# A hybrid attention layer with the compressed branch's padding to 128 taken out: 15-wide transposes and 15-row products in place of zero-filled 128-wide ones

## The chip, the cores and the metric

One core of one Trainium2 chip. The metric is the device time of one execution in microseconds (us). Of several executions the median counts.

## What is computed

One layer that is half block attention (MoBA, 8 heads) and half NSA attention (8 heads in 2 groups), on 256 tokens of width 2048, all in float32. With 256 tokens there is a single MoBA block, and the four selection blocks of NSA are all taken, so both the selected and the window branch are plain causal attention over 256 keys. The third NSA branch attends to 15 compressed tokens. Cut to what matters here:

```python
h = rmsnorm(x, g_norm)
proj = jnp.einsum('bsd,de->bse', h, w_in)          # 2048 x 7704
# NSA: n_cmp = 15 compressed keys and values per group
k_c = compress_tokens(n_kc..., pe_ck, w_ck1, w_ck2)
v_c = compress_tokens(n_vc..., pe_cv, w_cv1, w_cv2)
s_c = jnp.einsum('bgrqd,bgnd->bgrqn', q_raw, k_c).astype(jnp.float32) * scale
p_c = masked_softmax(s_c, cmp_end[None, :] <= pos[:, None])
o_c = jnp.einsum('bgrqn,bgnd->bgrqd', p_c.astype(v_c.dtype), v_c)
...
return gates[..., 0:1] * o_c + gates[..., 1:2] * o_s + gates[..., 2:3] * o_w
...
y = jnp.concatenate([y_moba, y_nsa], axis=-1)
return x + jnp.einsum('bse,ed->bsd', y, w_out)     # then a last rmsnorm
```

## The kernel before

The kernel is written engine by engine: each of SyncE, GpSimd, TensorE, ScalarE and VectorE has its own list of instructions, in an order written out by hand, and they meet at semaphores.

**The large products.** The input projection has 15 chunks of 512 columns, each cut into 4 units of 4 x 128 contraction rows; the output projection has 4 chunks, 16 units. This makes 76 slots, and `unit(slot)` runs in each. The weights of a unit arrive by a 1 MB DMA in `w_raw`; ScalarE rounds them to `w_hi` (`hi`, line 683) two slots ahead, VectorE takes the rest as `w_lo` (`lo`, line 879), and TensorE runs three products for each pair of operands (`three_products`, lines 420 to 422): 24 matmuls of 512 columns in a slot. In `matmul(out, a, v)` the argument `a` is the stationary side, loaded into the array by a LDWEIGHTS, and `v` streams past it.

**The attention** hangs between these units. There are 24 jobs (`JOBS`): 16 for NSA, two per head (b = 0 the selected branch, b = 1 the window branch), in slots 20 to 35, and 8 for MoBA after that. A job goes through four slots:
- slot s: `scores(j)` on TensorE (lines 573, 574 and, for the compressed keys, 577) into bank `b_s`; `row_max(j)` on VectorE into `prob`.
- slot s+1: `exps(j)` on ScalarE (line 741), `normalise(j)` on VectorE.
- slot s+2: `prob_T(j)` on TensorE transposes the probabilities into bank `b_p`, 128 columns at a time (line 588): four transposes for an NSA job, three for a MoBA job; `prob_out(j)` on ScalarE copies them to `pT` (line 748).
- slot s+3, for the second job of a head: `values(j)` on TensorE multiplies with the values into bank `b_o` (line 616); `o_evac(j)` on VectorE copies the result out.

In `prob[:, j % 2]` columns 0 to 383 hold the two causal pieces and columns 384 to 398 the 15 compressed probabilities of the 128 queries of half b; columns 399 to 511 are zero padding. So the fourth transpose is 128 x 128 with 113 zero rows in its result, and the product with the compressed values (line 614) has a contraction of 128 of which 113 are zero; rows 15 to 127 of `vc` are zero as well. The zeros are written by GpSimd: `vc` and one half of `prob` at the start (lines 346, 347), the other half of `prob` before projection chunk 5 (line 366), since that half first holds the second-layer weights `w2`. The semaphore `pad_ok` says that they are there; TensorE waits for it before the first transpose and ScalarE before it writes `vc`.

TensorE's order in a slot is: the unit, a transpose round of a projection chunk (`round_`, line 406), `values`, `prob_T`, `scores`. [...] Before the attention some small products use a part of the array: `ck_unit` (line 514) and `gates` (line 551) have 32 stationary columns, `ck_layer2` (line 539) has 15, and the first transpose (line 647) has 16 rows.

Of the kernel before, what the change touches and what calls it, by code (L numbers as in the profile page):

```python
# [134 lines left out]
CK2_SLOT = [12, 18]  # L135
GATE_SLOT = 13
TP = 2 * CS
PAD_CHUNK = 5

Y_ROUNDS = {54: [(0, 0, 0)], 55: [(0, 0, 1)], 56: [(0, 1, 0)], 57: [(0, 1, 1)],  # L140
            62: [(1, 0, 0), (1, 0, 1)], 63: [(1, 1, 0), (1, 1, 1)]}
# [10 lines left out]
def build_layer(nc, x, positions, inv_freq, w_in, g_norm, pe_ck, pe_cv, w_ck1, w_ck2, w_cv1, w_cv2,  # L152
# [4 lines left out]
    with ExitStack() as ctx:  # L157
        def sb(name, shape, dt=F32):
            return ctx.enter_context(nc.sbuf_tensor(name, shape, dt))
# [20 lines left out]
        raw_e = sb("raw_e", [P, MT, CW])  # L180
        junk = raw_e[:, :, :].rearrange("p m c -> p (m c)").bitcast(BF16)

        prob = sb("prob", [P, 2, 4 * P])
        w2 = prob[:, 0, :].rearrange("p (v t d) -> p v t d", v=2, t=2)


        pT = sb("pT", [P, 2, 512])
# [13 lines left out]
        sel = sb("sel", [P, 32])  # L201
        gate, gate_j = sb("gate", [P, MT, NGATE]), sb("gate_j", [P, NH, 2, 4])
        hid_e, hidT = sb("hid_e", [P, 2, TP]), sb("hidT", [P, 2, 2, TP])
        kcT, vc = sb("kcT", [P, CS + P]), sb("vc", [P, NG, HD])
        ssy, rstdy = sb("ssy", [P, 2, MT, 2]), sb("rstdy", [P, 2, MT])
        ssf, ssf1, rstdf = sb("ssf", [P, MT, 4]), sb("ssf1", [P, MT]), sb("rstdf", [P, MT])

# [15 lines left out]
        ident_ok, consts_ok, pool_step = sem("ident_ok"), sem("consts_ok"), sem("pool_step")  # L223
        sel_ok, xlo_even, rstd_ok, rope_sum, y_done = sem("sel_ok"), sem("xlo_even"), sem("rstd_ok"), sem("rope_sum"), sem("y_done")
        rstdy_ok, rstdf_ok = sem("rstdy_ok"), sem("rstdf_ok")
        gmul, pad_ok = sem("gmul"), sem("pad_ok")

        crows_T, x_round, unit_used, t_round = sem("crows_T"), sem("x_round"), sem("unit_used"), sem("t_round")
        ck_used, ck_sum, ck2_done = sem("ck_used"), sem("ck_sum"), sem("ck2_done")
# [91 lines left out]
        @block.gpsimd  # L321
        def _(pool):
            steps = [0]

            def link(ins):

                steps[0] += 1
                ins.then_inc(pool_step, 1)
                pool.wait_ge(pool_step, steps[0])


            link(nc.gpsimd.memset(ident[:, :], 0.0))
            nc.gpsimd.affine_select(out=ident[:, :], in_=ident[:, :], compare_op=ALU.not_equal, fill=1.0, base=0,
                                    pattern=[[-1, P]], channel_multiplier=1).then_inc(ident_ok, 1)
            nc.gpsimd.memset(half_c[:, :], -0.5)
            link(nc.gpsimd.memset(mask[:, :], 0.0))
            for c0, n, step, base in ((0, P, -1, 0), (2 * P, P, -1, 0), (3 * P, NCMP, -CS, 1 - CL), (3 * P + 16, NCMP, -CS, P + 1 - CL)):
                nc.gpsimd.affine_select(out=mask[:, c0:c0 + n], in_=mask[:, c0:c0 + n], compare_op=ALU.is_ge, fill=NEG,
                                        base=base, pattern=[[step, n]], channel_multiplier=1).then_inc(consts_ok, 1)
            link(nc.gpsimd.memset(sel[:, :], 0.0))  # L340
            for n in range(4):
                link(nc.gpsimd.affine_select(out=sel[:, :], in_=sel[:, :], compare_op=ALU.not_equal, fill=1.0, base=-32 * n,
                                             pattern=[[-1, 32]], channel_multiplier=1))
            nc.gpsimd.memset(kcT[:, TP:], 0.0).then_inc(sel_ok, 1)
            nc.gpsimd.memset(KV8[:, D:], 0.0).then_inc(sel_ok, 1)
            nc.gpsimd.memset(vc[:, :, :], 0.0).then_inc(pad_ok, 1)
            nc.gpsimd.memset(prob[:, 1, 3 * P + NCMP:], 0.0).then_inc(pad_ok, 1)

            for r in range(0, 8, 2):
                q, m = r // 2, r % 2  # L350
                pool.wait_ge(xhi_done, r + 1)
                nc.gpsimd.tensor_tensor(xT_lo[:, q * UK:(q + 1) * UK, m * P:(m + 1) * P],
                                        x_buf(r),
                                        xT_hi[:, q * UK:(q + 1) * UK, m * P:(m + 1) * P].bitcast(F32),
                                        ALU.subtract).then_inc(xlo_even, 1)

            pool.wait_ge(sq_done, 2)
            link(nc.gpsimd.tensor_scalar(ssx[:, :], ssx[:, :], 1.0 / D, EPS, ALU.mult, ALU.add))
            nc.gpsimd.tensor_tensor(rstd[:, :], ssx[:, :], half_c[:, :], ALU.pow).then_inc(rstd_ok, 1)
            pool.wait_ge(rstd_ok, 1)  # L360
            nc.gpsimd.tensor_scalar(nrstd[:, :], rstd[:, :], -1.0, None, ALU.mult).then_inc(rstd_ok, 1)

            for i, kind in enumerate(KINDS[:NC]):
                if i == PAD_CHUNK:
                    pool.wait_ge(ck2_done, 2)
                    nc.gpsimd.memset(prob[:, 0, 3 * P + NCMP:], 0.0).then_inc(pad_ok, 1)
                if kind in ROPED:
                    w = 2 * HD if kind == "kv" else CW
                    for m in range(MT):
                        pool.wait_ge(dve_read, dve_reads(i - 1) + 2 * (m + 1))  # L370
                        nc.gpsimd.tensor_tensor(rope_a[:, m, 0:w], rope_a[:, m, 0:w], rope_b[:, m, 0:w],  # L371
                                                ALU.add).then_inc(rope_sum, 1)
                elif kind == "z":
                    n = CHUNKS[i][2]
                    z = (rope_a, rope_b)[n % 2]
                    if n == 0:
                        pool.wait_ge(o_out, 2 * NH)
                    for m in range(MT):
                        pool.wait_ge(dve_read, dve_reads(i - 1) + m + 1)
                        nc.gpsimd.tensor_tensor(xo[:, m, n * CW:(n + 1) * CW], xo[:, m, n * CW:(n + 1) * CW],  # L380
                                                z[:, m, :], ALU.mult).then_inc(y_done, 1)
                    if n % 2:
                        h = n // 2
                        pool.wait_ge(y_sq, 4 * (h + 1))
                        link(nc.gpsimd.tensor_tensor(rstdy[:, h, :], ssy[:, h, :, 0], ssy[:, h, :, 1], ALU.add))
                        link(nc.gpsimd.tensor_scalar(rstdy[:, h, :], rstdy[:, h, :], 1.0 / HW, EPS, ALU.mult, ALU.add))
                        nc.gpsimd.tensor_tensor(rstdy[:, h, :], rstdy[:, h, :], half_c[:, :], ALU.pow).then_inc(rstdy_ok, 1)

            pool.wait_ge(gfin_in, 16)
            for c in range(3):  # L390
                for m in range(MT):
                    pool.wait_ge(fin_sq, 2 * c + m + 1)
                    nc.gpsimd.tensor_tensor(acc[:, m, c * CW:(c + 1) * CW], acc[:, m, c * CW:(c + 1) * CW],  # L393
                                            g_fin[:, c * CW:(c + 1) * CW], ALU.mult).then_inc(gmul, 1)
            pool.wait_ge(ssf_ok, 2)
            for m in range(MT):
                pool.wait_ge(fin_sq, 7 + m)
                one = slice(m, m + 1)
                link(nc.gpsimd.tensor_scalar(ssf1[:, one], ssf[:, m, 3:4], 1.0 / D, ssf1[:, one], ALU.mult, ALU.add))
                nc.gpsimd.tensor_tensor(rstdf[:, one], ssf1[:, one], half_c[:, one], ALU.pow).then_inc(rstdf_ok, 1)  # L400

        @block.tensor
        def _(pe):
# [177 lines left out]
            def prob_T(j):  # L581
                pe.wait_ge(prob_ready, j + 1)
                if j:
                    pe.wait_ge(pt_out, j)
                if j == 0:
                    pe.wait_ge(pad_ok, 3)
                for n in range(4 if JOBS[j][1] == "nsa" else 3):
                    last = nc.tensor.transpose(b_p[:, n * P:(n + 1) * P], prob[:, j % 2, n * P:(n + 1) * P], ident[:, :])  # L588
                last.then_inc(pt_done, 1)

            def values(j):
# [10 lines left out]
                for m in range(MT):  # L602
                    prods = []
                    if kind == "moba":
                        for kt in range(m + 1):
                            prods.append((pT[:, j % 2, (m + kt) * P:(m + kt + 1) * P], mv[:, kt, h * HD:(h + 1) * HD]))
                    else:
                        g = h // 4
                        for br in range(2):
                            jb = j - 1 + br  # L610
                            for kt in range(m + 1):
                                prods.append((pT[:, jb % 2, (m + kt) * P:(m + kt + 1) * P], nv[:, br, kt, g * HD:(g + 1) * HD]))
                        jb = j - 1 + m
                        prods.append((pT[:, jb % 2, 3 * P:4 * P], vc[:, g, :]))
                    for n, (a, v) in enumerate(prods):
                        last = nc.tensor.matmul(b_o[:, m * P:(m + 1) * P], a, v, start=n == 0, stop=n == len(prods) - 1)  # L616
                last.then_inc(pv_done, 1)
# [60 lines left out]
        def _(act):  # L678
# [65 lines left out]

            def prob_out(j):
                act.wait_ge(pt_done, j + 1)
                n = (4 if JOBS[j][1] == "nsa" else 3) * P
                nc.scalar.activation(pT[:, j % 2, 0:n], b_p[:, 0:n], ACT.Copy).then_inc(pt_out, 1)  # L748

            def quarters_out(n):  # L750

# [9 lines left out]

            def ck2_evac(kv):
                act.wait_ge(ck2_done, kv + 1)
                if kv:
                    act.wait_ge(pad_ok, 2)
                if kv == 0:
                    nc.scalar.activation(kcT[:, 0:TP], b_o[:, 0:TP], ACT.Copy).then_inc(ck2_out, 1)
                else:
# [392 lines left out]
```

## Time and profile before

| what | value |
|---|---|
| median of 3 executions | 517.62 us (517.52 to 518.07) |
| profiled execution, whole | 517.52 us |
| its span, first to last instruction | 515.7 us |
| TensorE matmul (PE) busy | 504.7 us, 98% |
| VectorE (DVE) busy | 292.7 us, 57% |
| ScalarE (ACT) busy | 238.5 us, 46% |
| GpSimd (POOL) busy | 62.8 us, 12% |
| mean granted TensorE clock | 0.996 of full |

The whole time is 1.8 us more than the span; that difference lies outside the kernel's instructions. PE is the matmul row, PEld the weight loads, which overlap it. Ends of matmuls are modelled, so what is read of PE below is the distance between the starts of neighbouring records, not their durations.

### The profile page before, as it was taken

How to read it: one execution, taken by the hardware profiler on the slowest of the kernel's cores; microseconds unless marked ns; L12 is line 12 of the kernel's file. 1: busy time of each engine (PE TensorE's matmuls, PEld its weight loads, DVE VectorE, ACT ScalarE, POOL GpSimd, SP SyncE). 2: the span in 40 equal slices, each digit the busy share in tenths (PEclk: the TensorE clock that was granted, in tenths of full speed). 3: DMA queues.
4: the chain of work that ended last, by engine and by line, in shares of the span. 5: the costliest groups of instructions: out<-in, count | busy, mean ns of one | idle time of the engine just before them, and what ended most of it. 6: DMA issues, size and time to landing. Idle time of an engine off the chain costs nothing.

```text
span 515.7 us, 6584 instructions
## 1 busy us (share of the span) xinstructions
PE 504.7 (98%) x2616; PEld 419.3 (81%) x2616; DVE 292.7 (57%) x512; ACT 238.5 (46%) x346; POOL 62.8 (12%) x69
## 2 busy tenths in 40 slices
PE   7999999999999999999999999999999999999993
PEld 6878777777888888888888888888888888888882
DVE  3797343445364766665665675555366666645541
ACT  3685343334445454364445444545463552545421
POOL 3210101001020300300012030001131030011020
PEclk9999999999999999999999999999999999999998
DMA  8898579584435244344334334443985457265313
GB/s 287 290 299 313 181 256 343 201 325 164 163 129 198 83 163 165 102 143 160 128 122 163 101 145 164 164 163 125 370 303 170 161 177 241 85 244 205 123 42 122
DMA packets 53903, 96.46 MB, mean 187 GB/s; under 512 B 4240, under 2 KB 13040, under 8 KB 53488
## 3 DMA queue, kind: packets, MB, share of 16 engines
q1 hardware_dynamic: 50688, 95.43, 53.0%
q10 hardware_dynamic: 3184, 0.61, 0.6%
q8 instruction: 21, 0.34, 0.3%
q14 instruction: 10, 0.08, 0.0%
HBM read 93.93 MB, written 2.10 MB: 186 GB/s over the span
## 4 chain that ended last, share of the span: by engine, by line
PE 97%; DMA 1%; DVE 0%; ACT 0%; DVEq 0%; POOLq 0%; issue 0%; SPq 0%; POOL 0%
PE proj L420 27%; PE proj L422 27%; PE proj L421 27%; PE b_o L616 4%; PE b_t L406 2%; PE b_s L574 2%; PE b_p L588 2%; PE b_s L514 2%; PE b_s L573 1%; DMA xo<-in_x_dram 1%; PE b_t L640 1%; PE b_s L577 1%; PE b_o L551 1%; PE b_o L406 0%; PE b_p L406 0%; PE b_o L539 0%
## 5 line engine op out<-in xcount | busy, mean ns | idle before, releaser
L879 DVE TENSOR_TENSOR w_lo<-w_raw,w_hi 128x2048 fp32r<-128x2048 f32 x72 | 167.0, 2322 | 103.6 <-ACT w_hi L683 103.1
L420 PE MATMUL proj<-w_hi,xT_hi 128*128 128x512 f32 x536 | 215.2, 401 | 0.1
L422 PE MATMUL proj<-w_hi,xT_lo 128*128 128x512 f32 x536 | 209.6, 391 | 0.0
L421 PE MATMUL proj<-w_lo,xT_hi 128*128 128x512 f32 x536 | 209.1, 390 | 0.0
L683 ACT ACTIVATE w_hi<-w_raw 128x2048 fp32r<-128x2048 f32 x72 | 137.4, 1910 | 44.4 <-PE proj L422 35.4
L420 PEld LDWEIGHTS proj<-w_hi,xT_hi 128*128 128x128 f32 x536 | 100.8, 188 | 22.8 <-issue 3.4
L422 PEld LDWEIGHTS proj<-w_hi,xT_lo 128*128 128x128 f32 x536 | 100.7, 188 | 21.5
L421 PEld LDWEIGHTS proj<-w_lo,xT_hi 128*128 128x128 f32 x536 | 101.0, 188 | 19.5
L371 POOL TENSOR_TENSOR rope_a<-rope_a,rope_b 128x512 f32<-128x512 f32 (+1 forms) x16 | 26.2, 1661 | 243.0 <-DVE rope_b L949 243.0
L735 ACT ACTIVATE Q<-b_t 128x512 f32<-128x512 f32 x18 | 10.8, 598 | 62.0 <-PE b_t L406 62.0
L748 ACT ACTIVATE pT<-b_p 128x512 f32<-128x512 f32 (+1 forms) x24 | 13.4, 557 | 53.8 <-PE b_p L588 53.8
L741 ACT ACTIVATE prob<-prob,nmx 128x128 f32<-128x128 f32 (+2 forms) x64 | 25.8, 407 | 0.2 <-DVE nmx L995 0.2
L991 DVE CUSTOM_DVE_ANT_0 prob<-b_s,mask 128x128 f32<-128x128 f32 (+2 forms) x64 | 16.7, 307 | 15.5 <-PE b_s L577 10.5
L420 PE MATMUL proj<-w_hi,ymT_hi 128*128 128x512 f32 x64 | 25.0, 391 | 0.0
L422 PE MATMUL proj<-w_hi,ymT_lo 128*128 128x512 f32 x64 | 25.0, 390 | 0.0
L421 PE MATMUL proj<-w_lo,ymT_hi 128*128 128x512 f32 x64 | 24.9, 390 | 0.0
L1004 DVE TENSOR_SCALAR coef<-sums 128x3 f32<-128x3 f32 (+1 forms) x24 | 4.5, 187 | 26.1 <-ACT prob L741 26.1
L1009 DVE TENSOR_SCALAR prob<-prob,coef 128x128 f32<-128x128 f32 (+2 forms) x64 | 15.5, 295 | 0.8
L380 POOL TENSOR_TENSOR xo<-xo,rope_a 128x512 f32<-128x512 f32 x4 | 7.2, 1812 | 70.6 <-DVE xo L1016 54.2
L1016 DVE COPY xo<-b_o 128x256 f32<-128x256 f32 x16 | 6.8, 422 | 15.2 <-PE b_o L616 15.2
L393 POOL TENSOR_TENSOR Q<-Q 128x512 f32<-128x512 f32 x6 | 7.6, 1291 | 62.6 <-ACT raw_e L790 62.6
L790 ACT ACTIVATE raw_e<-Q 128x512 bf16<-128x512 f32 x8 | 5.0, 631 | 21.6 <-DVE Q L1056 21.3
(163 smaller groups left out, 438.9 us busy)
## 6 DMA issues: line engine op xcount, KB each, us to landing
w_raw<-in_w_in_dram SPq DMA_DIRECT2D x57, 1024.0 KB, 4.9
w_raw<-in_w_out_dram SPq DMA_DIRECT2D x16, 1024.0 KB, 5.0
xo<-in_w_ck_dram SPq DMA_DIRECT2D x4, 1024.0 KB, 5.7
xo<-in_w_cv_dram SPq DMA_DIRECT2D x4, 1024.0 KB, 5.5
w_raw<-in_w_in_dram SPq DMA_DIRECT2D x12, 256.0 KB, 6.8
Q<-in_x_dram SPq DMA_DIRECT2D x1, 2048.0 KB, 10.1
out_dram<-Q SPq DMA_DIRECT2D x4, 512.0 KB, 3.2
xo<-in_x_dram SPq DMA_DIRECT2D x3, 512.0 KB, 8.0
```

Source lines behind the costliest of these rows:

```text
L371: nc.gpsimd.tensor_tensor(rope_a[:, m, 0:w], rope_a[:, m, 0:w], rope_b[:, m, 0:w], ALU.add).then_inc(rope_sum, 1)
L420: nc.tensor.matmul(dst, a_hi, b_hi, start=first, stop=False)
L421: nc.tensor.matmul(dst, a_hi, b_lo, start=False, stop=False)
L422: return nc.tensor.matmul(dst, a_lo, b_hi, start=False, stop=last)
L616: last = nc.tensor.matmul(b_o[:, m * P:(m + 1) * P], a, v, start=n == 0, stop=n == len(prods) - 1)
L683: nc.scalar.activation(split_of(u)[0], w_raw[:, u % RAW], ACT.Copy).then_inc(hi_ready, 1)
L735: nc.scalar.activation(dst, src, ACT.Copy).then_inc(t_out, 1)
L741: last = nc.scalar.activation(prob[:, b, c0:c1], prob[:, b, c0:c1], ACT.Exp, bias=nmx[:, b, n:n + 1], scale=SCALE, accum_out=sums[:, b, n: ...
L748: nc.scalar.activation(pT[:, j % 2, 0:n], b_p[:, 0:n], ACT.Copy).then_inc(pt_out, 1)
L879: nc.vector.tensor_tensor(wl, w_raw[:, u % RAW], wh.bitcast(F32), ALU.subtract).then_inc(lo_ready, 1)
L991: nc.vector.tensor_tensor_reduce(out=prob[:, j % 2, c0:c1], in0=b_s[:, c0:c1], in1=mask[:, k0:k0 + c1 - c0], scale=1.0, scalar=NEG, op0=AL ...
L1009: last = nc.vector.tensor_scalar(prob[:, j % 2, c0:c1], prob[:, j % 2, c0:c1], coef[:, j % 2, i:i + 1], None, ALU.mult)
```

## The change

The padding goes. `prob` shrinks from 2 x 512 to 2 x 400 columns (`w2` then lies across both halves, long before the first job), `vc` from 128 to 16 partitions, the three GpSimd fills go with the semaphore `pad_ok` and every wait on it. In an NSA job the fourth transpose takes 15 columns of `prob` and writes 15 partitions of `b_p`. `prob_out` becomes two copies for an NSA job: 128 partitions x 384, and 15 partitions x 128. The product with `vc` gets a contraction of 15 in place of 128. Nothing of the arithmetic result changes: what is left out was multiplied by zero.

```diff
-        prob = sb("prob", [P, 2, 4 * P])
+        prob = sb("prob", [P, 2, 400])
-        w2 = prob[:, 0, :].rearrange("p (v t d) -> p v t d", v=2, t=2)
+        w2 = prob[:, :, :].rearrange("p a b -> p (a b)")[:, 0:4 * HD].rearrange("p (v t d) -> p v t d", v=2, t=2)
...
-        kcT, vc = sb("kcT", [P, CS + P]), sb("vc", [P, NG, HD])
+        kcT, vc = sb("kcT", [P, CS + P]), sb("vc", [16, NG, HD])
...
-            nc.gpsimd.memset(vc[:, :, :], 0.0).then_inc(pad_ok, 1)
-            nc.gpsimd.memset(prob[:, 1, 3 * P + NCMP:], 0.0).then_inc(pad_ok, 1)
...
-                if i == PAD_CHUNK:
-                    pool.wait_ge(ck2_done, 2)
-                    nc.gpsimd.memset(prob[:, 0, 3 * P + NCMP:], 0.0).then_inc(pad_ok, 1)
...
-                if j == 0:
-                    pe.wait_ge(pad_ok, 3)
-                for n in range(4 if JOBS[j][1] == "nsa" else 3):
+                for n in range(3):
                     last = nc.tensor.transpose(b_p[:, n * P:(n + 1) * P], prob[:, j % 2, n * P:(n + 1) * P], ident[:, :])
+                if JOBS[j][1] == "nsa":
+                    last = nc.tensor.transpose(b_p[0:NCMP, 3 * P:4 * P], prob[:, j % 2, 3 * P:3 * P + NCMP], ident[:, :])
...
-                        prods.append((pT[:, jb % 2, 3 * P:4 * P], vc[:, g, :]))
+                        prods.append((pT[0:NCMP, jb % 2, 3 * P:4 * P], vc[0:NCMP, g, :]))
...
-                n = (4 if JOBS[j][1] == "nsa" else 3) * P
-                nc.scalar.activation(pT[:, j % 2, 0:n], b_p[:, 0:n], ACT.Copy).then_inc(pt_out, 1)
+                last = nc.scalar.activation(pT[:, j % 2, 0:3 * P], b_p[:, 0:3 * P], ACT.Copy)
+                if JOBS[j][1] == "nsa":
+                    last = nc.scalar.activation(pT[0:NCMP, j % 2, 3 * P:4 * P], b_p[0:NCMP, 3 * P:4 * P], ACT.Copy)
+                last.then_inc(pt_out, 1)
...
             def ck2_evac(kv):
                 act.wait_ge(ck2_done, kv + 1)
-                if kv:
-                    act.wait_ge(pad_ok, 2)
```

TensorE's list at the first `values`, in slot 24, before (`b_o` is the values' bank, `b_p` that of the transposes, `b_s` that of the scores; a row is output, stationary or streamed inputs, shape of the output):

```order
L616 MATMUL b_o<-nv,pT 128x128 x2
L616 MATMUL b_o<-vc,pT 128x128
L616 MATMUL b_o<-nv,pT 128x128 x4
L616 MATMUL b_o<-vc,pT 128x128
L588 MATMUL b_p<-ident,prob 128x128 x4
L573 MATMUL b_s<-Q 128x128
L574 MATMUL b_s<-Q 128x256
L577 MATMUL b_s<-kcT,Q 128x128
```

The same place with the change:

```order
L610 MATMUL b_o<-nv,pT 128x128 x2
L610 MATMUL b_o<-vc,pT 128x128
L610 MATMUL b_o<-nv,pT 128x128 x4
L610 MATMUL b_o<-vc,pT 128x128
L580 MATMUL b_p<-ident,prob 128x128 x3
L582 MATMUL b_p<-ident,prob 15x128
L567 MATMUL b_s<-Q 128x128
L568 MATMUL b_s<-Q 128x256
L571 MATMUL b_s<-kcT,Q 128x128
```

No instruction of TensorE moves or goes. The two `vc` products keep their output and lose 113 rows of contraction, which the rows don't show, and each stands between products that use the whole array. [...]

ScalarE's list in a slot with an NSA job, before (`w_hi` is the rounding of a unit's weights, for two slots later):

```order
L741 ACTIVATE prob,sums<-prob,nmx 128x128
L741 ACTIVATE prob,sums<-prob,nmx 128x256
L741 ACTIVATE prob,sums<-prob,nmx 128x15
L748 ACTIVATE pT<-b_p 128x512
L683 ACTIVATE w_hi<-w_raw 128x2048
```

And with the change:

```order
L735 ACTIVATE prob,sums<-prob,nmx 128x128
L735 ACTIVATE prob,sums<-prob,nmx 128x256
L735 ACTIVATE prob,sums<-prob,nmx 128x15
L741 ACTIVATE pT<-b_p 128x384
L743 ACTIVATE pT<-b_p 15x128
L677 ACTIVATE w_hi<-w_raw 128x2048
```

One copy has become two, ahead of the next rounding. It is so 16 times. GpSimd's list loses its three fills and is otherwise the same; VectorE's and SyncE's are the same.

## Rows read from the trace of the kernel before

**Rows 1.** The page: busy time, and the chain that ended last.

```profile
PE 504.7 (98%) x2616; PEld 419.3 (81%) x2616; DVE 292.7 (57%) x512; ACT 238.5 (46%) x346; POOL 62.8 (12%) x69
...
PE 97%; DMA 1%; DVE 0%; ACT 0%; DVEq 0%; POOLq 0%; issue 0%; SPq 0%; POOL 0%
```

**Rows 2.** Waits of PE, all of them: total us, times, longest.

```profile
PE b_t L640 <- POOL ident L333: 1.5, 1, 1.5
PE b_s L406 <- DMA xo<-in_x_dram: 0.8, 1, 0.8
PE b_o L406 <- DMA xo<-in_x_dram: 0.6, 1, 0.6
```

**Rows 3.** Busy time by stage: window; PE, PEld, DVE, ACT, POOL; clock, DMA share.

```profile
148.00:297.00 149.00, 149.00 (x819) 128.49 (x818) 94.19 (x276) 73.52 (x158) 14.06 (x8) 1.00 0.40 137
```

**Rows 4.** PE in order of time, ends of slots 22 and 23 (start us, us, what).

```profile
163.06 0.60 PE L406 MATMUL b_t<-ident,raw_e 128*128 128x128 f32 x4
163.50 0.60 PE L588 MATMUL b_p<-ident,prob 128*128 128x128 f32 x4
163.93 0.39 PE L573 MATMUL b_s<-Q 128*128 128x128 f32 x2
164.16 0.60 PE L574 MATMUL b_s<-Q 128*128 128x256 f32 x2
164.59 0.39 PE L577 MATMUL b_s<-kcT,Q 128*128 128x128 f32 x2
164.73 0.48 PE L420 MATMUL proj<-w_hi,xT_hi 128*128 128x512 f32 x1
165.04 0.40 PE L421 MATMUL proj<-w_lo,xT_hi 128*128 128x512 f32 x1
165.28 0.40 PE L422 MATMUL proj<-w_hi,xT_lo 128*128 128x512 f32 x1
...
170.74 0.60 PE L588 MATMUL b_p<-ident,prob 128*128 128x128 f32 x4
```

**Rows 5.** PE in order of time, the first values, slot 24.

```profile
178.16 0.61 PE L616 MATMUL b_o<-nv,pT 128*128 128x128 f32 x4
178.61 0.39 PE L616 MATMUL b_o<-vc,pT 128*128 128x128 f32 x2
178.83 1.06 PE L616 MATMUL b_o<-nv,pT 128*128 128x128 f32 x8
179.72 0.39 PE L616 MATMUL b_o<-vc,pT 128*128 128x128 f32 x2
179.95 0.60 PE L588 MATMUL b_p<-ident,prob 128*128 128x128 f32 x4
```

**Rows 6.** PE in order of time, where line 539's 15-wide products stand.

```profile
136.51 0.60 PE L406 MATMUL b_t<-ident,raw_e 128*128 128x128 f32 x4
137.04 1.04 PE L539 MATMUL b_o<-prob,hidT 128*15 128x128 f32 x8
138.02 0.50 PE L420 MATMUL proj<-w_hi,xT_hi 128*128 128x512 f32 x1
138.35 0.39 PE L421 MATMUL proj<-w_lo,xT_hi 128*128 128x512 f32 x1
```

**Rows 7.** PE in order of time, around line 514's 32-wide products.

```profile
53.78 0.39 PE L422 MATMUL proj<-w_hi,xT_lo 128*128 128x512 f32 x1
54.09 1.10 PE L514 MATMUL b_s<-xo,KV 128*32 128x256 f32 x16
55.13 0.50 PE L420 MATMUL proj<-w_hi,xT_hi 128*128 128x512 f32 x1
55.47 0.39 PE L421 MATMUL proj<-w_lo,xT_hi 128*128 128x512 f32 x1
55.70 0.40 PE L422 MATMUL proj<-w_hi,xT_lo 128*128 128x512 f32 x1
...
124.56 0.50 PE L420 MATMUL proj<-w_hi,xT_hi 128*128 128x512 f32 x1
124.89 0.39 PE L421 MATMUL proj<-w_lo,xT_hi 128*128 128x512 f32 x1
```

**Rows 8.** PE in order of time, the 16-row transpose near the start.

```profile
6.50 0.63 PE L406 MATMUL b_o<-ident,xo 128*128 128x128 f32 x2
...
6.71 0.42 PE L406 MATMUL b_o<-ident,xo 128*128 128x128 f32 x1
7.07 0.28 PE L647 MATMUL b_p<-ident,pT 16*128 16x16 f32 x1
```

**Rows 9.** Loads of line 616: min, median, max ns, first and last start.

```profile
L616 PEld LDWEIGHTS b_o<-vc,pT x32: 191/192/193, 178.5 to 289.1; 128*128 128x128 f32 x32
```

**Rows 10.** PE groups by shape: busy us, mean ns, idle before.

```profile
L616 PE MATMUL b_o<-vc,pT 128*128 128x128 f32 x32 | 6.2, 276 | 0.0
L514 PE MATMUL b_s<-xo,KV 128*32 128x256 f32 x128 | 8.8, 393 | 0.0
L539 PE MATMUL b_o<-prob,hidT 128*15 128x128 f32 x8 | 1.0, 274 | 0.0
```

**Rows 11.** ACT groups by shape: busy us, mean ns, idle before and its releaser.

```profile
L748 ACT ACTIVATE pT<-b_p 128x512 f32<-128x512 f32 x16 | 9.5, 591 | 30.8 <-PE b_p L588 30.8
L748 ACT ACTIVATE pT<-b_p 128x384 f32<-128x384 f32 x8 | 3.9, 489 | 23.1 <-PE b_p L588 23.1
L769 ACT ACTIVATE vc<-b_o 15x256 f32<-15x256 f32 x1 | 0.4, 372 | 0.4 <-PE b_o L539 0.4
```

**Rows 12.** ACT in order of time, slot 23.

```profile
165.36 0.57 ACT L748 ACTIVATE pT<-b_p 128x512 f32<-128x512 f32 x1
165.84 1.91 ACT L683 ACTIVATE w_hi<-w_raw 128x2048 fp32r<-128x2048 f32 x1
```

**Rows 13.** DVE in order of time, slot 23.

```profile
167.77 2.29 DVE L879 TENSOR_TENSOR w_lo<-w_raw,w_hi 128x2048 fp32r<-128x2048 f32 x1
```

**Rows 14.** POOL in order of time, its fills and what follows.

```profile
4.60 0.31 POOL L346 MEMSET vc<- 128x256 f32 x1
4.85 0.19 POOL L347 MEMSET prob<- 128x113 f32 x1
9.03 1.29 POOL L352 TENSOR_TENSOR xT_lo<-rope_a,xT_hi 128x512 fp32r<-128x512 f32 x1 [3.99 <-ACT xT_hi L693]
```

More of the change, by code:

```diff
@@ L137 @@
 TP = 2 * CS
-PAD_CHUNK = 5
 Y_ROUNDS = {54: [(0, 0, 0)], 55: [(0, 0, 1)], 56: [(0, 1, 0)], 57: [(0, 1, 1)],
@@ L225, in build_layer @@
         rstdy_ok, rstdf_ok = sem("rstdy_ok"), sem("rstdf_ok")
-        gmul, pad_ok = sem("gmul"), sem("pad_ok")
+        gmul = sem("gmul")
         crows_T, x_round, unit_used, t_round = sem("crows_T"), sem("x_round"), sem("unit_used"), sem("t_round")
```

## The prediction

> **What bounds the kernel now.** I read the page first. PE is busy in 98% of the span, and the chain that ended last is PE for 97% [rows 1]. That alone doesn't say that PE is at its limit, since a busy PE can be a slow one, so I read its waits next: three, 2.9 us in all, each in the first microseconds [rows 2]. [...] The question is what the new shapes do to the distance between PE's starts.
>
> **The yardstick.** Two regular stretches give it. Four transposes take 0.44 us, from 163.06 to 163.50, so 0.11 us each [rows 4]. Records of line 616 are as far apart: eight in 0.89 us, two of `vc` in 0.22 us [rows 5]. From the last pair of a 128-wide fp32 product to the second matmul of the next unit it is 0.45 us (164.59 to 165.04) [rows 4]. Rounded matmuls of 512 columns follow each other at 0.23 us (55.47 to 55.70) [rows 7].
>
> **The fewer rows and columns by themselves: 0.** A product with 15 stationary columns is in the trace. Line 539 streams 128 columns past 15, as the new transpose does. Its eight records last 1.04 us together [rows 6] and 0.27 each [rows 10], so their starts are (1.04 - 0.27) / 7 = 0.11 us apart, as at full width, (1.06 - 0.28) / 7 [rows 5, 10]. So nothing is gained by the width; the streamed columns pace it, and these stay 128 in all new instructions. Fewer contraction rows change neither the streamed columns nor the 128 loaded ones, whose load takes 192 ns now [rows 9], beside the matmul ahead. I take 0 for the work itself, in both.
>
> **The passage to a part of the array and back: the term that decides.** Before, all these instructions use the whole array. [...] The trace has such passages for column groups. In: four transposes and the step to line 539 take 0.53 us (136.51 to 137.04) [rows 6] where they take 0.44 elsewhere [rows 4], 0.09 more. Ahead of line 514 the step is 0.31 us in place of 0.23, 0.08 more [rows 7]. Out: six records of line 539 at 0.11 put its last pair at 137.70, and from there to line 421 it is 0.65 us [rows 6] in place of 0.45 [rows 4], 0.20 more. That 0.20 has two halves: 138.02 to 138.35 is 0.33 in place of 0.23, so 0.10 for a 128-column weight load that no longer hides behind the matmul ahead of it, and 0.10 until the array is empty. After line 514 it is the same at its first visit, 55.13 to 55.47 being 0.34, and at its last, 124.56 to 124.89 being 0.33 [rows 7]; with 16 records a visit its 128 [rows 10] are eight visits, and line 539 the ninth.
>
> For a `vc` product I add it up so. In: 0.09 to empty the array, and 0.11 since its own 128-column load is now in the open (line 539 had only 15 columns to load and so shows the 0.09 alone). Its two records then run at the usual distance. Out: 0.20. Together 0.40 us, and 16 x 0.40 = **6.4 us**. A row group in place of a column group is seen only once, at 7.07 us: 0.36 us from the transpose ahead, where that one had come 0.21 after its neighbour (6.50, 6.71) [rows 8], so 0.15 more, at a time when all starts were twice as far apart as later. This suggests that a passage to a row group isn't free. Bounds for one product: 0.18 if only the two emptyings count, 0.56 if both loads lie open in full (2 x 0.09 + 2 x 0.19 [rows 9]); for 16 this is 2.9 to 9.0 us. I take 6.4 because the nearest rows, the exits, show 0.20 each time.
>
> [...]
>
> **The 15-wide transposes: 0.** [...] If they did pass into a column mode, each would cost the 0.09 and 0.20 of line 539, 16 x 0.29 = 4.6 us more. [...]
>
> **ScalarE: 0.** The copy of 512 columns (591 ns) becomes one of 384 (489 ns) and one of 15 x 128. The latter isn't in the trace; 15 x 256 takes 372 ns, and 128 columns fewer are worth 591 - 489 = 102 ns, so I estimate 270 [rows 11]. Each NSA job then costs ScalarE 489 + 270 - 591 = 168 ns more, 2.7 us for 16. Behind it in the queue waits the rounding of the weights [rows 12], and behind that VectorE's `w_lo`, which is done at 170.06 [rows 13]. That is unit 25's, and TensorE starts unit 25 only behind the transposes and scores that follow the `values` of slot 24, after 180.4 us [rows 5]; 10 us of slack hide 0.2. `pT` of this job, done at 165.93, is read at 178.16; that of the head's second job comes a slot of 7.24 us later (163.50 to 170.74 [rows 4]) and has 5 us. Were this cover gone, it would cost up to 2.7 us.
>
> **GpSimd and the waits: 0.** The first two fills end at 5.04 us, and then GpSimd stands idle for 3.99 us until ScalarE's `xT_hi` [rows 14]; the third fill, as long as the second (0.19 us), falls in an engine that is 12% busy [rows 1]. No wait on `pad_ok` is among PE's waits [rows 2]. ScalarE's and TensorE's waits on it were met long before. Moving the tensors behind `prob` to other addresses I count at nothing.
>
> **Sum.** 517.52 (profiled execution) + 6.4 = 523.9 us, against a span of 515.7 + 6.4 = 522.1. The median shown is 0.1 above the profiled execution, so I say **524.0 us**, 1.2% slower.
>
> **Rivals.**
> - *Both passages cost.* The 15-wide transposes drain the array too. For it: line 539 has the same shape and pays. [...] 524.0 + 4.6 = 528.6; if they also fell from one record to two, another 16 x 0.11 = 1.8, 530.4.
> - *The passage is cheap for rows.* The weights of a 15-row product touch only the first row group, and the load may slip in earlier than after a column passage; then only the emptyings count: 517.6 + 2.9 = 520.5.
> - *Nothing to pay: not slower.* TensorE might take a product on the first row group as a whole-array one whose other rows are idle, and run on without emptying. It then costs 0 and the time is 517.6. It decides from the point where the distance from `nv` to `vc` is again 0.11 us. Against it stand the 0.15 of [rows 8] and all nine column visits. That the time falls below 517.6 I give next to nothing, as no instruction of PE goes.
> - *ScalarE's second copy reaches PE.* Slack of 5 to 10 us speaks against it; 524.0 + 2.7 = 526.7 at most.
>
> [...]
>
> **Chances.** The forecast 0.66, with its own range 523 to 525.5; both passages (528.6 or more) 0.15; cheap rows 0.08; nothing to pay 0.07; ScalarE 0.02; faster 0.02. The range 520.5 to 529.0 takes in the two middle rivals and the bounds of the passage (2.9 gives 520.5, 9.0 gives 526.6) and leaves out the free case and the second record. About 0.2% is what a measurement of this kernel can tell from no change: slower by more has 0.91, within 0.2% 0.07, faster 0.02.
>
> **What the profile of the changed kernel would show.** In the first `values` block, 1.79 us long from `nv` to the transposes (178.16 to 179.95) [rows 5], I expect 2.6 us, with 0.20 from the last `nv` record to `vc`, 0.22 from the first to the second `vc` record and 0.20 to the next. The 15-wide transpose should stand 0.11 from its neighbours on both sides; 0.20 there means the first rival. PE's waits stay three. Wrong would prove: PE waiting for `pT` or `w_lo`, or a `vc` product 0.11 after `nv`.

## The result

The changed kernel takes 524.08 us (median of 4, 523.86 to 524.68), the kernel before 517.85 us (median of 4, 517.52 to 518.56). The ratio is 1.0117, with a 95% interval from 1.0106 to 1.013: 1.2% slower. The forecast was 524.0 us.

### The profile page after: what moved, and what is told of

It is laid out like the page before. It is cut to its first block, busy times and chain, and to the rows that moved or that the text cites. A ratio compares the mean times of both kernels' runs of the same rounds, so it can differ in the third digit from the quotient of the medians.

```text
span 522.9 us, 6595 instructions
## 1 busy us (share of the span) xinstructions
PE 511.9 (98%) x2616; PEld 422.1 (81%) x2616; DVE 292.9 (56%) x512; ACT 239.2 (46%) x362; POOL 62.1 (12%) x66
## 4 chain that ended last, share of the span: by engine, by line
PE 95%; DVE 2%; DMA 1%; ACT 1%; issue 0%; POOLq 0%; SPq 0%; POOL 0%; DVEq 0%
PE proj L414 26%; PE proj L416 26%; PE proj L415 26%; PE b_o L610 5%; PE b_t L400 2%; PE b_s L568 2%; PE b_p L580 2%; PE b_s L508 2%; PE b_t L634 1%; PE b_s L567 1%; DMA xo<-in_x_dram 1%; PE b_s L571 1%; PE b_o L545 1%; DVE w_lo L878 1%; DVE w_lo L873 0%; PE b_p L582 0%
## 5 line engine op out<-in xcount | busy, mean ns | idle before, releaser
L741 ACT ACTIVATE pT<-b_p 128x384 f32<-128x384 f32 x24 | 11.7, 487 | 59.2 <-PE b_p L582 35.5
```

Of the source, the lines that this page charges most:

```text
L741: last = nc.scalar.activation(pT[:, j % 2, 0:3 * P], b_p[:, 0:3 * P], ACT.Copy)
```

## The profile after

The page of the changed kernel, busy time and the first line of the chain that ended last, to be held against [rows 1]:

```profile
PE 511.9 (98%) x2616; PEld 422.1 (81%) x2616; DVE 292.9 (56%) x512; ACT 239.2 (46%) x362; POOL 62.1 (12%) x66
...
PE 95%; DVE 2%; DMA 1%; ACT 1%; issue 0%; POOLq 0%; SPq 0%; POOL 0%; DVEq 0%
```

PE runs the same 2616 matmul records and is busy for 7.2 us more; ScalarE has 16 instructions more and 0.7 us more work, GpSimd three fills fewer. The span is 522.9 us. The chain is 2% DVE and 1% ACT where [rows 1] had 0%: mostly work at 21 to 32 us, such as the following line, long before the change acts. PE waits for none of it, as its list of waits shows.

```profile
26.48 2.93 DVE w_lo L878 x3
```

PE's waits are as few as in [rows 2], and none is new:

```profile
PE b_t L634 <- POOL ident L332: 1.5, 1, 1.5
PE b_s L400 <- DMA xo<-in_x_dram: 0.6, 1, 0.6
PE b_o L400 <- DMA xo<-in_x_dram: 0.6, 1, 0.6
```

So PE works longer at the same instructions. Where, is seen at the first `values`, PE in order of time (start us, us, instruction, records). Of the kernel before, what followed the block of [rows 5]:

```profile
180.38 0.39 PE L573 MATMUL b_s<-Q 128*128 128x128 f32 x2
```

And the changed kernel:

```profile
179.52 0.61 PE L610 MATMUL b_o<-nv,pT 128*128 128x128 f32 x4
180.06 0.48 PE L610 MATMUL b_o<-vc,pT 15*128 15x128 f32 x2
180.48 1.16 PE L610 MATMUL b_o<-nv,pT 128*128 128x128 f32 x8
181.56 0.48 PE L610 MATMUL b_o<-vc,pT 15*128 15x128 f32 x2
181.98 0.55 PE L580 MATMUL b_p<-ident,prob 128*128 128x128 f32 x3
182.36 0.27 PE L582 MATMUL b_p<-ident,prob 128*15 128x128 f32 x1
182.47 0.39 PE L567 MATMUL b_s<-Q 128*128 128x128 f32 x2
```

From the first `nv` record to the scores it was 2.22 us (178.16 to 180.38) and is 2.95 us: 0.73 us more for a head with two `vc` products. An instruction of line 616 or 610 shows as two records (32 for the 16 with `vc`, [rows 10]), a transpose as one (16 for the 16 of line 582). Every step can be read:
- Four `nv` records and the way in take 0.54 us (179.52 to 180.06) where they took 0.45: 0.09.
- Two `vc` records and the way out take 0.42 (180.06 to 180.48) where they took 0.22: 0.20, which is 0.10 for the first weight load in the open and 0.10 for the emptying. The two records last 0.48 us together, against 0.39 before.
- Eight `nv` records and the second way in take 1.08 (180.48 to 181.56) where they took 0.89: 0.19, another open load and another emptying.
- Two `vc` records and the way out to the transposes: 0.42 again, 0.19 more than the 0.23 before.
- Three transposes take 0.38 (181.98 to 182.36) in place of 0.33: the open load of a transpose is worth only 0.05.
- The 15-wide transpose takes 0.11 (182.36 to 182.47), as the 128-wide one did. It makes no passage.

Eight heads at 0.73 are 5.8 us. That the load lies in the open is read from the weight loads (PEld). Before the change, the loads of the first two `vc` records began 0.11 us ahead of their products (178.61):

```profile
178.50 0.30 PEld L616 LDWEIGHTS b_o<-vc,pT 128*128 128x128 f32 x2
```

In the changed kernel they begin together with them (180.06):

```profile
180.06 0.29 PEld L610 LDWEIGHTS b_o<-vc,pT 15*128 15x128 f32 x2
182.25 0.10 PEld L582 LDWEIGHTS b_p<-ident,prob 128*15 128x15 f32 x1
```

The load of the 15-wide transpose begins 0.11 us ahead of it (182.36), so it stays hidden. The rest of each step, 0.09 to 0.10 us more between the last product ahead of a passage and the first behind it, I call the emptying; the rows show its length, not what happens in it.

ScalarE's two copies, as groups by shape (busy us, mean ns, idle before and its releasers), against [rows 11]:

```profile
L741 ACT ACTIVATE pT<-b_p 128x384 f32<-128x384 f32 x24 | 11.7, 487 | 59.2 <-PE b_p L582 35.5 <-PE b_p L580 23.7
L743 ACT ACTIVATE pT<-b_p 15x128 f32<-15x128 f32 x16 | 4.0, 251 | 0.0
```

The copy of 15 x 128 takes 251 ns, and no PE instruction waits for it. It overlaps the copy ahead of it, so it delays ScalarE by much less: in slot 24 the rounding of the weights starts 0.55 us after the first copy (182.67 to 183.22), where it started 0.50 after the single one (180.58 to 181.08). Sixteen times 0.05 is 0.8 us, near the 0.7 that ScalarE's busy time gained.

**What the two profiled executions differ in besides.** Their spans are 7.2 us apart, not 5.8. The other 1.3 us lie before the first product of the input projection, which starts at 11.64 us in the kernel before and at 12.96 in the changed one; nothing was changed there that PE waits for. From that product to the end of the span it is 504.1 us before and 509.9 after, 5.8 more. From the chain in order of time, the stretch of small products with which TensorE fills the time before its first unit, before and after:

```profile
7.35 4.53 PE b_t L640 x30
```

```profile
7.31 5.89 PE b_t L634 x30
```

It is the same list of 128-wide products. In both executions their starts are 0.21 us apart at first and 0.11 later, and only the moment of the step from one to the other differs: 9.4 us in the kernel before, 12.1 in the changed one. Thirteen records at 0.10 us more each are the 1.3 us. So the stage from 9.5 to 12 us has 24 records at work in one, the first of the next unit among them, and 14 in the other:

```profile
9.50:12.00 2.50, 2.50 (x24) 2.46 (x23) 2.50 (x4) 2.05 (x4) 0.82 (x1) 1.00 1.06 401
```

```profile
9.50:12.00 2.50, 2.50 (x14) 2.50 (x13) 2.50 (x4) 2.01 (x4) 0.77 (x1) 1.00 1.06 399
```

(Busy time by stage: window; PE, PEld, DVE, ACT, POOL with their instructions; clock, DMA share, GB/s.) In the ten profiled executions of this study this stretch lasts 4.53 to 5.89 us, and the two just shown are its ends: the kernel before was profiled with the shortest start of all and the changed one with the longest. In four experiments with the operation list of the kernel before up to slot 20 it lasts 4.64, 5.45, 5.27 and 5.70 us (e1, e5, e6 and e7 below), so it varies between executions and isn't the change's. The medians are 6.2 us apart, 0.4 more than the trace gives to the change; the varying start is large enough for that, but the executions without a profile don't show theirs. The granted clock in these two rows reads 1.00 in both, so they don't show why the records were at first twice as far apart; that stays open.

## The experiments

Each is compared with runs of the kernel before on the same chip. My theory was that the whole loss is the `vc` products' passages to one row group and back. A row group or a column group is my name, here and in the texts on record, for a part of the array's rows or columns; no run shows how an instruction names such a part or where one ends. What I call a visit is one way in and one way out.

### Only the products: e1

```diff
-                        prods.append((pT[:, jb % 2, 3 * P:4 * P], vc[:, g, :]))
+                        prods.append((pT[0:15, jb % 2, 3 * P:4 * P], vc[0:15, g, :]))
```

> The kernel before, with one edit: the 16 products with vc contract over 15 rows instead of 128; transposes, copies, fills and the size of prob stay. Theory (each of these products is a passage to a row group and back): the whole loss of the change is here, 16 products at about 0.36 us as the changed kernel's records show them (0.73 us a head), so 5.8 us over the kernel before, near 523.6. Rival (the loss comes from the two copies, the narrow transposes, the new addresses or the missing fills): the time of the kernel before, within 0.5 us.

Measured: 523.71 us (523.48 to 524.12) against 518.05; ratio 1.0108, interval 1.0093 to 1.0123. PE in order of time at the first `values`:

```profile
178.40 0.61 PE L616 MATMUL b_o<-nv,pT 128*128 128x128 f32 x4
178.94 0.48 PE L616 MATMUL b_o<-vc,pT 15*128 15x128 f32 x2
179.35 1.16 PE L616 MATMUL b_o<-nv,pT 128*128 128x128 f32 x8
180.44 0.48 PE L616 MATMUL b_o<-vc,pT 15*128 15x128 f32 x2
180.85 0.66 PE L588 MATMUL b_p<-ident,prob 128*128 128x128 f32 x4
181.34 0.39 PE L573 MATMUL b_s<-Q 128*128 128x128 f32 x2
```

2.94 us from `nv` to the scores, as in the changed kernel, with the padding, the four full transposes and the single copy all in place. One edit in one line brings the whole loss: 5.7 us by the medians, and 5.8 with the start left out, as in the changed kernel (table below).

### Only the rest: e2

The changed kernel with the products back at 128 rows:

```diff
-        kcT, vc = sb("kcT", [P, CS + P]), sb("vc", [16, NG, HD])
+        kcT, vc = sb("kcT", [P, CS + P]), sb("vc", [P, NG, HD])
...
+            nc.gpsimd.memset(vc[:, :, :], 0.0).then_inc(pad_ok, 1)
+            nc.gpsimd.memset(pT[:, 1, 3 * P:], 0.0).then_inc(pad_ok, 1)
...
-                        prods.append((pT[0:NCMP, jb % 2, 3 * P:4 * P], vc[0:NCMP, g, :]))
+                        prods.append((pT[:, jb % 2, 3 * P:4 * P], vc[:, g, :]))
```

> The changed kernel with the vc products back at 128 rows of contraction (vc zero-filled to 128 partitions again, pT's unused rows filled once at the start): the other half of the change alone, with its 15-wide transposes, two copies per NSA job and smaller prob. Theory: the distance of the 15-wide transpose to both neighbours stays 0.11 us, ScalarE's second copy stays hidden, and the time is that of the kernel before, within 0.5 us. Rival (the transposes or the second copy cost something): 16 x 0.29 = 4.6 us more for a passage, or up to 2.7 us for the copies.

Measured: 518.28 us against 518.05; ratio 1.0, interval 0.999 to 1.0009. PE in order of time after the first `values`:

```profile
180.72 0.49 PE L584 MATMUL b_p<-ident,prob 128*128 128x128 f32 x3
181.05 0.27 PE L586 MATMUL b_p<-ident,prob 128*15 128x128 f32 x1
181.16 0.39 PE L569 MATMUL b_s<-Q 128*128 128x128 f32 x2
```

0.33 for three transposes and 0.11 for the narrow one. The narrow transposes, the second copy and the smaller `prob` cost nothing together, within 0.5 us. Two GpSimd fills and the waits on them are back here, so their absence isn't tested by e2; that the changed kernel's PE has no new wait speaks for it. With e1 this splits the change cleanly: one half has all of it, the other nothing.

### Is it any contraction under 128 rows: e5 and e6

The edit of e1 with 80 and with 64 in place of 15; the rows beyond 15 are zeros. I estimated the time of the kernel before for 80 rows, and for 64 rows the loss of 15 rows, 5.8 us; if the price went with the size of the part, 64 rows would lose between 0 and 3 us.

> The kernel before with the vc products over 80 rows (65 of them zero) instead of 128. [...] Rival (a contraction under 128 costs by itself): part or all of 5.8 us, near 523.6.

> [...] Theory: the passage costs whenever the set of groups changes, however many are named, so the same as 15 rows, 5.8 us over the kernel before. [...]

Measured: 80 rows 518.51 us, ratio 1.0005 (0.9996 to 1.0015); 64 rows 523.79 us, ratio 1.0109 (1.0094 to 1.0124). PE in order of time, with 80 rows:

```profile
179.60 0.39 PE L616 MATMUL b_o<-vc,pT 80*128 80x128 f32 x2
179.82 1.06 PE L616 MATMUL b_o<-nv,pT 128*128 128x128 f32 x8
```

And with 64:

```profile
179.42 0.48 PE L616 MATMUL b_o<-vc,pT 64*128 64x128 f32 x2
179.84 1.16 PE L616 MATMUL b_o<-nv,pT 128*128 128x128 f32 x8
```

Two records and the step behind them take 0.22 us with 80 rows and 0.42 with 64, the same as with 15. A contraction shorter than 128 isn't by itself what costs: 15 and 64 rows pay alike, and 80 rows pay nothing; no run took a number between 64 and 80, and none shows why the price differs between them.

### The price is per visit: e3

The changed kernel with the two `vc` products of a head side by side:

```diff
-                        prods.append((pT[0:NCMP, jb % 2, 3 * P:4 * P], vc[0:NCMP, g, :]))
+                        prods.insert(0 if m else len(prods), (pT[0:NCMP, jb % 2, 3 * P:4 * P], vc[0:NCMP, g, :]))
```

> The changed kernel with the second vc product of a head moved ahead of the four nv products of its half, so that the head's two vc products stand side by side: the same instructions, 8 visits to the row group instead of 16. Theory (the price is per visit, two emptyings of 0.09 us and two open loads of 0.10): a head costs 0.38 us instead of 0.73, so 8 x 0.35 = 2.8 us less than the changed kernel, near 521.3. Rival (the price is per 15-row product, for example a slower load or stream): the time of the changed kernel, 524.1.

Measured: 521.39 us (520.9 to 521.82) against 518.14, ratio 1.0061 (1.0047 to 1.0075), so 3.3 us over the kernel before where the changed kernel is 6.2 (with the start left out, 3.1 and 5.8). PE in order of time:

```profile
178.66 0.61 PE L610 MATMUL b_o<-nv,pT 128*128 128x128 f32 x4
179.21 0.71 PE L610 MATMUL b_o<-vc,pT 15*128 15x128 f32 x4
179.84 1.16 PE L610 MATMUL b_o<-nv,pT 128*128 128x128 f32 x8
180.84 0.49 PE L580 MATMUL b_p<-ident,prob 128*128 128x128 f32 x3
```

Four `vc` records and the way out take 0.63 us: the second pair of records adds 0.21 to the 0.42 of the first, so 0.11 a record and nothing for a passage. Half the visits, half the loss.

### A passage where the narrow transpose stands: e4

The changed kernel with each 15-wide transpose replaced by an ordinary fp32 product of the same operands, the probabilities stationary and the identity streamed; the result is the same, and each product shows as two records (`x2` below) in place of one:

```diff
-                    last = nc.tensor.transpose(b_p[0:NCMP, 3 * P:4 * P], prob[:, j % 2, 3 * P:3 * P + NCMP], ident[:, :])
+                    last = nc.tensor.matmul(b_p[0:NCMP, 3 * P:4 * P], prob[:, j % 2, 3 * P:3 * P + NCMP], ident[:, :], start=True, stop=True)
```

> [...] Theory (passages cost the same to a column group as in the rows of lines 514 and 539, and the transposes of the change don't make one): each costs 0.09 in, 0.11 for the second record, 0.20 out, 0.40 us, so 16 x 0.40 = 6.4 us over the changed kernel, near 530.5. Rival (the 15-wide transposes already pay a passage that is hidden in the change's loss): only the second record, 16 x 0.11 = 1.8 us, near 525.9.

Measured: 530.59 us (530.4 to 530.77), ratio to the kernel before 1.0239 (1.0225 to 1.0252). PE in order of time:

```profile
182.36 0.55 PE L580 MATMUL b_p<-ident,prob 128*128 128x128 f32 x3
182.84 0.39 PE L582 MATMUL b_p<-ident,prob 128*15 128x128 f32 x2
183.16 0.49 PE L567 MATMUL b_s<-Q 128*128 128x128 f32 x2
183.49 0.38 PE L568 MATMUL b_s<-Q 128*128 128x256 f32 x1
```

The same shape, `128*15`, now pays: 0.48 to it in place of 0.38, 0.32 for its two records and the way out, 0.33 for the next pair in place of 0.22. 530.59 is 6.5 us over the changed kernel's 524.08, which makes 0.41 for each of the 16 (with the start left out 6.3 us, 0.40 each). So a narrow product does make a column visit in this place and a narrow transpose does not, though the trace writes both as `128*15`.

### Fewer streamed columns: e7

```diff
-                    last = nc.tensor.matmul(b_s[:, 3 * P:4 * P], Q[:, Q_RAW + h, b * P:(b + 1) * P],
-                                            kcT[:, (h // 4) * CS:(h // 4) * CS + P], start=True, stop=True)
+                    last = nc.tensor.matmul(b_s[:, 3 * P:3 * P + NCMP], Q[:, Q_RAW + h, b * P:(b + 1) * P],
+                                            kcT[:, (h // 4) * CS:(h // 4) * CS + NCMP], start=True, stop=True)
```

> The kernel before with the compressed scores (line 577) streaming 15 columns of kcT instead of 128; both sides still use the whole array, and the 113 columns left out were never read. [...] Rival (time follows the streamed columns): 32 x 0.05 to 0.10 us, 1.6 to 3.2 us less. A passage would show as a loss of some 5.8 us.

Measured: 518.55 us against 518.14, ratio 1.0003 (0.9993 to 1.0013). No gain that can be measured, where my estimate was 0 to 0.6 us. The pair of records lasts 0.29 us in place of 0.39, but the stationary side is still 128 columns wide:

```profile
182.27 0.29 PE L577 MATMUL b_s<-kcT,Q 128*128 128x15 f32 x2
```

From this pair to the next unit it is 0.14 us (182.27 to 182.41), as it was (181.04 to 181.18). The weight loads didn't move either. First this run's, then those of the kernel before:

```profile
182.05 0.41 PEld L577 LDWEIGHTS b_s<-kcT,Q 128*128 128x128 f32 x2
182.38 0.19 PEld L420 LDWEIGHTS proj<-w_hi,xT_hi 128*128 128x128 f32 x1
```

```profile
180.83 0.41 PEld L577 LDWEIGHTS b_s<-kcT,Q 128*128 128x128 f32 x2
181.15 0.19 PEld L420 LDWEIGHTS proj<-w_hi,xT_hi 128*128 128x128 f32 x1
```

So 15 streamed columns leave the starts where 128 had them. Whether the loads set the pace here isn't shown, since no run made the load narrower at the same 15 columns.

### The same lesson used on the kernel before: e8

The kernel before has visits of its own: eight for line 514. Two blocks in one slot make four of them.

```diff
-CK_SLOT = [6, 7, 9, 10, 12, 13, 15, 16]
-CK_AT = {s: c for c, s in enumerate(CK_SLOT)}
+CK_SLOT = [7, 7, 10, 10, 13, 13, 16, 16]
+CK_AT = {s: [c for c in range(8) if CK_SLOT[c] == s] for s in CK_SLOT}
...
-                if slot in CK_AT:
-                    ck_unit(CK_AT[slot])
+                for c in CK_AT.get(slot, []):
+                    ck_unit(c)
```

> The kernel before with its 8 blocks of 32-column products (line 514) put two to a slot, in slots 7, 10, 13 and 16 instead of 6, 7, 9, 10, 12, 13, 15 and 16; their weights are fetched in pairs likewise. Same instructions, 4 column visits fewer. Theory: a visit costs 0.09 in and 0.20 out, 0.29 us, so 4 x 0.29 = 1.2 us less than the kernel before, near 516.9, if the paired fetches come in time. Rival (the two fetches side by side delay a block or a unit's weights): TensorE waits for them in slots 7 to 16, a new wait of its own in the trace, and the gain is gone or a loss of 1 to 10 us stands in its place.

Measured: 516.81 us (median of 9, 516.05 to 517.33) against 518.24; ratio 0.9975, interval 0.9965 to 0.9985. It is 1.4 us faster than the kernel before by the medians, 1.3 by the ratio, and so the fastest of all. PE in order of time:

```profile
59.79 1.97 PE L514 MATMUL b_s<-xo,KV 128*32 128x256 f32 x32
61.69 0.50 PE L420 MATMUL proj<-w_hi,xT_hi 128*128 128x512 f32 x1
62.03 0.39 PE L421 MATMUL proj<-w_lo,xT_hi 128*128 128x512 f32 x1
```

Two blocks in one take 1.90 us to the next unit, where one took 1.04 (54.09 to 55.13 in [rows 7]); the second adds 0.86 and no passage. PE's waits stay three, all in the first microseconds, so the fetches come in time. A visit of line 514 is worth more than the 0.29 us that I expected: 0.08 on the way in, 1.04 - 0.86 = 0.18 within and behind the block, 0.10 for the load behind it, 0.36 together. Four are 1.4 us. With the start left out the two profiled executions differ by 1.7; the 0.3 above that stays open.

**All runs with the start left out.** The times vary by up to 2 us between executions of one kernel. Four profiled executions have the same work, within the 0.2 us of the table: the kernel before, e2, e5 and e7, at 517.52, 518.44, 518.56 and 518.70 us. Their stretch of filling products lasts 4.53, 5.38, 5.45 and 5.70 us, and the time less this stretch is 513.0 to 513.1 us in all four. So the start carries the variation, and a comparison of what lies between the first product of the projection and the end of the span is sharper than that of the medians (us, one profiled execution each):

| run | first product | end of span | between them | against before |
|---|---|---|---|---|
| kernel before | 11.64 | 515.7 | 504.1 | |
| changed kernel | 12.96 | 522.9 | 509.9 | +5.8 |
| e1, 15 rows alone | 11.82 | 521.7 | 509.9 | +5.8 |
| e2, the rest alone | 12.38 | 516.6 | 504.3 | +0.2 |
| e5, 80 rows | 12.57 | 516.8 | 504.2 | +0.1 |
| e6, 64 rows | 12.31 | 522.2 | 509.9 | +5.8 |
| e3, one visit a head | 12.11 | 519.3 | 507.2 | +3.1 |
| e4, a column passage | 12.70 | 529.0 | 516.3 | +12.2 |
| e7, 15 streamed columns | 12.76 | 516.9 | 504.2 | +0.1 |
| e8, paired blocks | 11.86 | 514.3 | 502.4 | -1.7 |

## Why the prediction held

- **PE is the limit from 148 to 297 us.** Held. The 16 NSA jobs lie there, and PE is busy for 149.00 of 149.00 us at a granted clock of 1.00, with DVE at 94.19 and ACT at 73.52 us [rows 3]; so what a PE instruction takes more stands in the total. The loss of e1 shows in full in the time, with nothing absorbed: 8 heads at 0.72 us are 5.8, and so is the difference in the table.
- **The work itself: 0.** Held for both: the 15-wide transpose stands 0.11 us from its neighbours, and so do records on 15 rows once the visit has begun (e3) and records on 80 rows (e5). That the streamed columns pace the records was my reading of the rows; with 256 of them two records take 0.43 us and with 128 two take 0.22 [rows 4, 5], but from 128 to 15 nothing is gained (e7).
- **The passages: 6.4 us, at 0.40 a product.** The passages are there, and the size was 10% too large. A product costs 0.36: a head costs 0.73 in place of 0.80. A visit between two `nv` stretches costs 0.39 (e3), near my 0.40: no run shows the 0.11 that I took for the load of the `vc` product on the way in; the first `vc` pair shows 0.10, its starts being 0.21 us apart in place of 0.11. The mis-sized part is the way out to the transposes, 0.14 to 0.15 us in place of 0.20, since I priced all ways out by line 539's exit to a 512-column product; eight such exits are 0.4 to 0.5 of the 0.6 us too much. The term measures 5.8 us in the trace and 5.7 by e1's medians. The way in, 0.09, is as read from the visits of lines 514 and 539; that a visit to 15 rows isn't free, [rows 8] could only suggest. Of the signs that I named, the distances came out: 0.20, 0.21 and 0.20 us around the first `vc` pair, 0.11 around the narrow transpose, three waits. The block up to the transposes is 2.46 us (179.52 to 181.98), not 2.6.
- **The bounds: 0.18 and 0.56 us a product.** Both were off. e6 pays on 64 rows as e1 does on 15, e5 on 80 rows pays nothing, and what I call the emptying is 0.09 to 0.10 us each way where there is a passage. The emptyings alone, without the open loads, give 2.9 us; the loads are the other half of the price. Of a load only 0.10 us shows, though its record lasts 0.18 to 0.19; the upper bound, both loads in the open in full, was far off. That the groups an instruction names decide on a passage was my assumption, and no run shows the groups.
- **The narrow transposes: 0.** Held (e2), and e4 shows that the rival was real for an ordinary product of that shape. Why the transpose makes no passage isn't shown.
- **ScalarE's second copy: 0.** Held. I estimated 270 ns and it takes 251. But the sum that made it 168 ns a job, 2.7 us in all, took the copies as if one began when the other ended; they overlap, and the delay is 0.05 us a job, 0.8 in all.
- **GpSimd, the waits, the addresses: 0.** Held. The addresses are within the 0.5 us of e2; for the fills and waits it follows from PE's unchanged waits and from the table, where the changed kernel loses no more than e1, which keeps them.
- **The rivals.** "Nothing to pay" and "cheap for rows" fall with e1 and e6, "both passages cost" with e2.
- **The total.** That 524.08 lies within 0.1 of 524.0 is luck: the term was 0.6 us too large, and the sum started from one of the shortest executions, 517.52, with the shortest start of all, while the medians of the kernel before in the comparisons are 517.85 to 518.24. From 517.62 with 5.8 us it would have been 523.4.

## What to carry to other kernels

In this kernel zero padding up to the full array was free: two `vc` records and the step behind them took 0.22 us on 128 rows as on 80, and 0.42 on 64 or 15; the 15-wide transpose took 0.11 us, as the 128-wide one did. Before cutting a matmul's shape, ask whether a product of the new shape makes a passage and what stands on both sides of it: here a single small product amid whole-array ones cost 0.36 us, more than its own 0.22. Where such small products are wanted, put them side by side; that alone took 2.7 us off the changed kernel and 1.4 us off the kernel before.

## What the runs showed of the hardware that I had not expected

- A product on 80 rows runs as on the whole array, one on 64 rows pays what one on 15 pays (0.42 us for two records and the way out, against 0.22).
- An fp32 transpose and an fp32 product can have the same shape in the trace, `128*15`, and differ in whether they make a passage: 0.11 us to the next instruction (e2) against 0.32 for the product's two records and the way out (e4).
- The first weight load behind a passage costs 0.10 us in front of an fp32 product and 0.05 in front of a transpose (three in 0.38 us in place of 0.33).
- The stretch of filling products at the start lasts from 4.53 to 5.89 us between the profiled executions, because its products go from 0.21 us apart to 0.11 at a different moment each time; a comparison of two single executions can mislead by up to 1.4 us.
- Records of products that use 32 of the array's columns follow each other closely: the second 16 of line 514 in e8 take 0.86 us, 0.05 each, where whole-array records with the same 256 streamed columns take 0.43 a pair, 0.22 each (164.16 to 164.59 in [rows 4]). No run here tests what they need for it.
